# A two-layer hybrid decoder trunk: the layer and unit loops, written out in the instruction streams or run as hardware loops

## The reference

```python
for l in range(DEPTH):
    h = rmsnorm(x, norm_w[l])
    proj = jnp.einsum('bld,dn->bln', h, w_in[l]).astype(f32)
    ...
    y_a = gdn_branch(...)        # gated DeltaNet, 8 heads of 128
    y_b = hgrn2_branch(...)      # HGRN2, 8 heads of 128
    y_c = s5_branch(...)         # S5 state space, 64 groups of 16 channels
    y_d = retention_branch(...)  # RetNet retention, 8 heads of 128
    branch = jnp.einsum('blcw,cwd->blcd', ys, w_branch[l]).astype(f32)
    gates = jax.nn.sigmoid(gate_logits.reshape(B, L, N_BRANCH, D_MODEL))
    merged = jnp.sum(gates * branch, axis=2)
    x = x + jnp.einsum('bld,de->ble', merged.astype(x.dtype), w_out[l])
return rmsnorm(x, final_norm_w)
```

## Time and profile before

| | before |
|---|---|
| time, median of 3 runs | 3149.24 us |
| profiled execution: its own time | 3147.71 us |
| profiled execution: span from first to last instruction | 3145.9 us |
| PE busy | 3036.6 us (97%), granted clock 0.995 |
| DVE busy | 2167.7 us (69%) |
| ACT busy | 1461.4 us (46%) |
| POOL busy | 270.1 us (9%) |

### The profile page before, as it was taken

The page is one execution under the profiler, slowest core; times in us unless marked ns, Lnnn a source line. Parts: engine busy times, 40 slices in busy tenths (PEclk is TensorE's granted clock), DMA queues, the critical chain, the costliest instruction groups (busy, mean ns, idle before and its releaser), DMA issues.

```text
span 3145.9 us, 50828 instructions
## 1 busy us (share of the span) xinstructions
PE 3036.6 (97%) x20316; PEld 2769.8 (88%) x20316; DVE 2167.7 (69%) x3300; ACT 1461.4 (46%) x2102; POOL 270.1 (9%) x512
## 2 busy tenths in 40 slices
PE   5999999999999999999989999999999999999998
PEld 5999999999998888888889999999999988888886
DVE  5877877887786555545558877877877865555554
ACT  4455355445536444444453555455355454444443
POOL 2012102101200000000011011012102000000000
PEclk9999999999999999999989999999999999999999
DMA  4455445455546666666634455455445566666655
GB/s 125 133 142 141 133 132 145 130 136 138 145 128 189 194 194 194 193 195 187 203 98 134 126 144 136 130 138 151 125 135 139 146 195 194 194 193 193 193 178 167
DMA packets 614108, 494.23 MB, mean 157 GB/s; under 512 B 18512, under 2 KB 496272, under 8 KB 613360
## 3 DMA queue, kind: packets, MB, share of 16 engines
q1 hardware_dynamic: 606800, 485.09, 53.7%
q0 software_dynamic: 6784, 4.70, 0.7%
q10 hardware_dynamic: 288, 1.18, 0.1%
HBM read 488.81 MB, written 2.10 MB: 156 GB/s over the span
## 4 chain that ended last, share of the span: by engine, by line
PE 43%; issue 24%; DVE 18%; DVEq 7%; ACT 6%; ACTq 2%; DMA 0%; SPq 0%; POOLq 0%; POOL 0%
PE PJ L1431 24%; PE S L1431 6%; DVE w_lo L969 5%; PE GA L1431 3%; PE RA L1431 3%; PE HA L1431 3%; PE GB L1431 2%; DVE region L1112 2%; DVEq L1087 2%; DVE work L1085 2%; ACT w_hi L553 2%; DVEq L1142 1%; DVEq L1137 1%; DVE mix L1065 1%; DVEq L1105 1%
## 5 line engine op out<-in xcount | busy, mean ns | idle before, releaser
L969 DVE TENSOR_TENSOR w_lo<-raw_w,w_hi 128x1024 fp32r<-128x1024 f32 x912 | 1115.6, 1224 | 767.6 <-ACT w_hi L553 742.6
L553 ACT ACTIVATE w_hi<-raw_w 128x1024 fp32r<-128x1024 f32 x912 | 964.3, 1059 | 822.4 <-PE PJ L1431 377.8
L1431 PE MATMUL PJ<-h_hi,w_hi 128*128 128x256 f32 x3584 | 1045.8, 292 | 0.0
L1431 PE MATMUL PJ<-h_hi,w_lo 128*128 128x256 f32 x3584 | 1015.2, 283 | 0.0
L1431 PE MATMUL PJ<-h_lo,w_hi 128*128 128x256 f32 x3584 | 1014.8, 283 | 0.0
L1431 PEld LDWEIGHTS PJ<-h_hi,w_hi 128*128 128x128 f32 x3584 | 688.0, 192 | 11.9 <-issue 11.9
L1431 PEld LDWEIGHTS PJ<-h_lo,w_hi 128*128 128x128 f32 x3584 | 688.4, 192 | 0.0
L1431 PEld LDWEIGHTS PJ<-h_hi,w_lo 128*128 128x128 f32 x3584 | 687.0, 192 | 0.0
L1431 PE MATMUL PJ<-w_hi,h_hi 128*128 128x512 f32 x640 | 249.2, 389 | 2.0 <-DVE h_lo L1363 2.0
L1431 PE MATMUL PJ<-w_hi,h_lo 128*128 128x512 f32 x640 | 249.0, 389 | 0.0
L1431 PE MATMUL PJ<-w_lo,h_hi 128*128 128x512 f32 x640 | 249.0, 389 | 0.0
(11 more groups left out here) (398 smaller groups left out, 4235.5 us busy)
## 6 DMA issues: line engine op xcount, KB each, us to landing
raw_w<-w_in SPq DMA_DIRECT2D x704, 512.0 KB, 3.7
raw_w<-w_branch SPq DMA_DIRECT2D x128, 512.0 KB, 4.2
raw_w<-w_out SPq DMA_DIRECT2D x64, 512.0 KB, 4.2
raw_w<-s_glu_w SPq DMA_DIRECT2D x16, 512.0 KB, 4.7
ret_decay<-c_ret POOLq DMA_DIRECT2D x16, 128.0 KB, 3.2
work<-final_norm_w SPq DMA_DIRECT2D x2, 1024.0 KB, 7.3
out<-x_tok SPq DMA_DIRECT2D x4, 512.0 KB, 2.9
x_tok<-x ACTq DMA_DIRECT2D x1, 1024.0 KB, 7.9
```

What stands on the lines that cost most here:

```text
L553: A_(w_hi[i % RING][:, :, :], raw_w[i % RING][:, :, :], ACT.Copy).then_inc(hi_ready, 1)
L969: TT(w_lo[i % RING][:, :, :], raw_w[i % RING][:, :, :], w_hi[i % RING][:, :, :].bitcast(f32), ALU.subtract).then_inc(raw_used[i % RING], 1)
L1431: return nc.tensor.matmul(o, w, m, start=start, stop=stop)
```

## The change

The Python loops over layers and over units become hardware loops on all five engines. The counts and offsets that were constants are now registers (`snap` puts an expression into one). The bodies are the same, and so is the work that is executed.

```diff
@@ SP
-            for l in range(DEPTH):
-                r0 = l * RAW_USES
+            with sp.Fori(0, DEPTH) as l:
+                r0 = sp.snap(l * RAW_USES)
...
-                for u in range(UNITS):
-                    base = r0 + u * USES
+                with sp.Fori(0, UNITS) as u:
+                    base = sp.snap(r0 + u * USES)
...
@@ ACT
-                for u in range(UNITS):
-                    n = l * UNITS + u
-                    n1 = n + 1
-                    s0, r0 = sl + u * HALVES, rl + u * USES
-                    ga0, gb0 = n * GA_N, n * GB_N
-                    ha0, sa0, cv0 = n * HA_N, n * SA_N, n * 3
+                with act.Fori(0, UNITS) as u:
+                    n = act.snap(l * UNITS + u)
+                    n1 = act.snap(n + 1)
+                    s0, r0 = act.snap(sl + u * HALVES), act.snap(rl + u * USES)
+                    ga0, gb0 = act.snap(n * GA_N), act.snap(n * GB_N)
+                    ha0, sa0, cv0 = act.snap(n * HA_N), act.snap(n * SA_N), act.snap(n * 3)
...
@@ PE
-                for u in range(UNITS):
+                with pe.Fori(0, UNITS) as u:
...
-                p0, pr, q0 = sl + POST_SPLIT0, rl + UNITS * USES, l * STEPS
+                p0, pr, q0 = pe.snap(sl + POST_SPLIT0), pe.snap(rl + UNITS * USES), pe.snap(l * STEPS)
```

More of the change, by code:

```diff
@@ L379, in _ @@
                         load(i, base, W[ds(l, 1), :, k0:k0 + HALF, ds(u * P + BLOCKS[i // 2], P)])
-                post = r0 + UNITS * USES
+                post = sp.snap(r0 + UNITS * USES)
                 def load_wide(i, source):
@@ L424, in _ @@
             pool.dma_start(log_dt[:, :], A["s5_log_dt"].rearrange("l (j g) -> (l j) g", g=2)).then_inc(s5_in, 16)
-            for l in range(DEPTH):
-                l1 = l + 1
+            with pool.Fori(0, DEPTH) as l:
+                l1 = pool.snap(l + 1)
                 pool.wait_ge(params_used, l1)
@@ L448, in _ @@
                 nc.gpsimd.tensor_tensor(x_rs[:, :], x_rs[:, :], mhalf[:, 0:2], ALU.pow).then_inc(rms_ready, 1)
-                for u in range(UNITS):
-                    n1 = l * UNITS + u + 1
+                with pool.Fori(0, UNITS) as u:
+                    n1 = pool.snap(l * UNITS + u + 1)
                     pool.wait_ge(bc_used, n1)
@@ L553, in split_hi @@
                 A_(w_hi[i % RING][:, :, :], raw_w[i % RING][:, :, :], ACT.Copy).then_inc(hi_ready, 1)
-            for l in range(DEPTH):
-                l1 = l + 1
-                sl, rl = l * SPLITS, l * RAW_USES
+            with act.Fori(0, DEPTH) as l:
+                l1 = act.snap(l + 1)
+                sl, rl = act.snap(l * SPLITS), act.snap(l * RAW_USES)
                 split_hi(0, sl, rl)
@@ L767, in _ @@
                     ahead(27)
-                p0, pr = sl + POST_SPLIT0, rl + UNITS * USES
-                q0 = l * STEPS
+                p0, pr = act.snap(sl + POST_SPLIT0), act.snap(rl + UNITS * USES)
+                q0 = act.snap(l * STEPS)
                 def ahead(j):
@@ L970, in split_lo @@
                    ALU.subtract).then_inc(raw_used[i % RING], 1)
[L972 to L975, removed]
+            with dve.Fori(0, DEPTH) as l:
+                l1 = dve.snap(l + 1)
+                a0 = dve.snap(l * 2)
+                sl = dve.snap(l * SPLITS)
                 mean_square(l1)
@@ L1049, in _ @@
                 dve.drain().then_inc(cols_ready, 1)
[L1051 to L1055, removed]
+                with dve.Fori(0, UNITS) as u:
+                    n = dve.snap(l * UNITS + u)
+                    n1 = dve.snap(n + 1)
+                    ga0, gb0, ha0 = dve.snap(n * GA_N), dve.snap(n * GB_N), dve.snap(n * HA_N)
+                    ra0, sa0, cv0 = dve.snap(n * RA_N), dve.snap(n * SA_N), dve.snap(n * 3)
                     def tap(m, k):
@@ L1068, in conv_taps @@
                         last.then_inc(conv_summed, 1)
-                    s0 = sl + u * HALVES
+                    s0 = dve.snap(sl + u * HALVES)
                     def ahead(i):
@@ L1339, in y_low @@
                     last.then_inc(y_lo_ready, 1)
-                p0, q0 = sl + POST_SPLIT0, l * STEPS
+                p0, q0 = dve.snap(sl + POST_SPLIT0), dve.snap(l * STEPS)
                 def ahead(j):
@@ L1447, in three_pass @@
                 return MM(o, wl, mh, False, last)
-            for l in range(DEPTH):
-                l1 = l + 1
-                sl, rl = l * SPLITS, l * RAW_USES
+            with pe.Fori(0, DEPTH) as l:
+                l1 = pe.snap(l + 1)
+                sl, rl = pe.snap(l * SPLITS), pe.snap(l * RAW_USES)
                 pe.wait_ge(params_in, l1 * (16 * 11))
@@ L1458, in _ @@
                 pe.wait_ge(diag_ready, l1)
-                x0 = l * (KT // 2)
+                x0 = pe.snap(l * (KT // 2))
                 def scale_x(i):
@@ L1492, in _ @@
                 MM(RA[:, 2 * UNITS:3 * UNITS], after, gate_g[:, 0, :]).then_inc(gc_written, 1)
[L1493 to L1498, removed]
+                with pe.Fori(0, UNITS) as u:
+                    n = pe.snap(l * UNITS + u)
+                    n1 = pe.snap(n + 1)
+                    pj0, ga0, gb0, ha0 = pe.snap(n * NB), pe.snap(n * GA_N), pe.snap(n * GB_N), pe.snap(n * HA_N)
+                    ra0, sa0, cv0 = pe.snap(n * RA_N), pe.snap(n * SA_N), pe.snap(n * 3)
+                    r0 = pe.snap(rl + u * USES)
                     def project(i):
```

## The result

The changed kernel takes 3240.78 us (median of 4 runs, 3238.36 to 3244.29) against 3149.53 us before (4 runs, 3147.71 to 3150.5): a ratio of 1.0287, 95% interval 1.0275 to 1.0299, so 91 us slower. The forecast was 3195 us, 46 us slower. The profiled execution took 3245.19 us, with a span of 3243.5 us, 97.6 us more than that of the kernel before. Its time is the second longest, and its mean granted clock of 0.988 the lowest, of 26 executions on record (3233.88 to 3245.33 us, clock 0.988 to 0.994), so what is read from its trace is some 4 us more than the median shows.

The account below looks back on a forecast made before the run. PE bounds the kernel, paced by DVE for some 47 us of each unit. Terms 29 + 3 + 2 + 10 + 4 = 48 us on 3147.71 gave 3196, forecast 3195 us; range 3154 to 3262, forecast's own 3180 to 3220.

Parts of the forecast that it names:

- rival 1: Unit starts: each code fetch exposed with 5 us on PE, or other engines late; 3257 us (3220 to 3290), chance 0.20.
- The register rows on DVE: L1094 to the second rotary part: register rows directly behind drains cost 1.8 us a unit, 29 us in all.
- counts from registers: Instructions waiting for a register's value cost extra at dispatch: 0.2 us, 3 us in all.
- PE's rows: Register rows on PE, covered by its sequencer's 2.0 us lead: nothing; without cover 3.5 us a unit.
- ACT and the table load: ACT, 504 to 527.6 us: moved load gains 0.2 us, two tap rows on DVE cost 0.3; 2 us in all.
- The way back: Branch to a unit's start: code fetch outlasts PE's lead, 0.7 us each, 15 times, 10 us.
- The cautious end of my forecast: Upper figure for PE's loss at each branch back to a unit's start: 2.0 us.
- Both delays run side by side, so the larger counts: Unit starts: PE's loss of 0.7 to 2.0 us and DVE's 0.5 us lateness overlap; 0.7 us taken.
- Layer starts: Serial stretch between engines at each layer's start, with branch and ISA rows: 2 us each, 4 us.
- Wide stage, SP and POOL: SP's loads wait for `w_lo`, POOL is ready 7.2 us early, wide stage has no idle to grow: nothing.
- my own signs against me: Wrong if units grow under 1 us, growth sits at their starts, or PE's busy time changes.
- rival 2: Unit loop's code is still held, no stall at the branch; 3184 us (3165 to 3190), chance 0.20.

Follow-up runs that it names:

- e6: Kernel before with DVE alone given the layer loop, its eight units written out, counts in registers; 3168.43 us, ratio 1.0069.
- e5: Changed kernel with the prefetch hint for the unit loop's closing branch on PE, DVE and ACT; 3183.50 us, ratio 1.0118.
- e4: Changed kernel with the unit loops of PE, DVE, ACT and POOL written out inside the layer loop; 3172.67 us, ratio 1.0075.
- e10: Kernel before with PE alone looped, with the prefetch hint for its unit loop's closing branch; 3151.32 us against 3148.64, ratio 1.0008.
- e8: Kernel before with ACT alone looped; 3147.81 us against 3147.07, ratio 1.0002.
- e1: Kernel before with PE's instruction stream alone looped, without a hint; 3203.92 us, ratio 1.0171.
- e3: Changed kernel with the prefetch hint for the unit loop's closing branch on PE alone; 3204.11 us, ratio 1.0176.
- e7: Kernel before with DVE alone looped over layers and units; 3196.77 us, ratio 1.0158.
- e12: Kernel before, no loop, with 45 already fulfilled waits on PE at the start of each unit but a layer's first; 3199.52 us, ratio 1.0159.
- e11: Kernel before, no loop, with 75 already fulfilled waits on PE at the start of each unit but a layer's first; 3268.45 us, ratio 1.0382.
- e2: Changed kernel with PE's stream written out, while DVE, ACT, POOL and SP loop; 3201.02 us, ratio 1.0168.

## Why the prediction was half right

The direction and the place of one half were right. The time was 46 us short and above the forecast's own range, 3180 to 3220 us, in that of rival 1, 3220 to 3290 us. Nearly all of the 46 us is one term of the sum. (The sum itself gave 3196 us on the profiled execution and so 3197 on the median, not 3195, and rival 1's 113 us make 3262 and not 3257; neither changes the account.)

*The register rows on DVE, 29 us, and counts from registers, 3 us.* Measured: 22 us for the rows of the counts (e6), and some 13 us, give or take 7, for the rows that the unit number adds (e5 less e4, 0.0043 of 3149), 35 us for the forecast's 32. That they come so close is in part luck. In the stretch that I had priced, the waits after `h_scores` and the rotary parts went from 31.1 to 50.1 us at PE, 19 us for my 29, and the 13 us lie mostly at the taps, outside that stretch. There is growth also in the GA of the decay (3.6 to 10.1 us), which I had not named. The rows themselves are 40 ns (ALU_OP) and 57 ns (FUSED_REGOPS, median) on DVE. Before L1128, where a FUSED_REGOPS row of 46 ns took the place of the semaphore's row of 21 ns, the idle time went from 3.0 to 3.6 us, 0.04 us for each of 16.

*PE's rows, nothing.* Right: at most 5 us (e10).

*ACT and the table load, +2 us.* Right as nothing: 0.6 us [-2 to 3] (e8). The win of 0.2 us a unit is there in e8's wait GB <- ACT region L631, 5.8 us for 8.5 in 16, but not in its time, and in the changed kernel this wait is 9.5. One thing was mis-sized: I had 0.3 us a unit for two rows between the taps. There are nine, and the idle time at them grew by 0.76 us a unit (22.0 against 9.8 us, over 16), counted above.

*The way back, 10 us: the step that failed in size.* I wrote "with some 0.3 us for branch and register rows and a lead of 2.0 us, PE loses between 0.7 and 2.0 us" and took 0.7 times 15. The form of this sum holds, and 14 times is the right count. The fetch is the wrong term: I took 2.4 us from the landing of an 8 KB load, where the branch with its fetch is 4.5 us. So it is 2.8 us each, 39 us, and 17 us more for what follows it (next part). The cautious end of my forecast, 2.0, lay below too, though the 5 us of rival 1 were above.

*What was missing.* The clock. Nowhere had I asked what PE's engine does after standing still. Eight stretches of half clock, 40.8 us: the matmuls follow each other there by 0.21 us in place of 0.12,

```profile
643.54 0.58 PE L1431 MATMUL PJ<-h_hi,w_hi 128*128 128x256 f32 x1 [2.88 <-issue]
643.92 0.41 PE L1431 MATMUL PJ<-h_lo,w_hi 128*128 128x256 f32 x1
644.13 0.41 PE L1431 MATMUL PJ<-h_hi,w_lo 128*128 128x256 f32 x1
644.35 0.41 PE L1431 MATMUL PJ<-h_hi,w_hi 128*128 128x256 f32 x1
```

so that at most 40.8 x (1 - 0.12/0.21) = 17 us are lost in this execution. With the stops that is 56 us for the 10 of the forecast, and e1 less e10 says 51 on the chip.

*"Both delays run side by side, so the larger counts."* Right, and the runs show it: PE alone looped costs 54 us, DVE alone 50, together 104; less the 13.7 us that show at GB only once PE's stop is gone (e3), 90, which is the 91 measured. DVE was later than my 0.5 us, with two stops, but hidden.

*Layer starts, 4 us.* Half of it: the first GB of layer 1 comes at 66.06 in place of 65.01 us, and from the last S matmul of the wide stage to the first GB of layer 2 it is 39.25 us in place of 38.49, together 1.8 us. No row stood behind my 2 us each. From the first GB of the eighth unit to the wide stage it is 2.2 us more in layer 1 and 2.5 us in layer 2, with no way back in between. *Wide stage, SP and POOL, nothing.* Right.

The sum as measured: 35 on DVE, 39 for stops, 17 for the clock, 2 for the layers is 93 us, against 97.6 of the spans. Rival 1 came nearest in time (3257 us), and of its two forms it was the fetch on PE, not the late engines. Of my own signs against me, two of three came: the growth sits at the units' starts for more than half, and PE's busy time changed.

The Trainium skill, page "Runtime: NRT & Kernel Launch", section "Instruction fetch mechanics", says that a taken branch to a page outside the current two stalls on a fetch. The trace agrees for PE (4.5 us) and DVE (3.0 us behind the branch). ACT's next row came after 0.2 us, and the packets fit that: with ACT alone looped (e8) q14 has 16 between 200 and 900 us for 23 before, with DVE alone looped (e7) 41. ACT's unit has 188 rows in the trace and is not fetched again, DVE's has 312 and is. The same section of the Trainium skill also says that prefetch is purely sequential and only two lines are held. The hinted loop contradicts that: 700 us without a packet on q8, over more than six units of some 1800 instructions each. My rival 2, code that is held, is thus right for a loop with a hint and wrong for one without. Why the same code is fetched again without a hint was not tried.

## What to carry to other kernels

Price a hardware loop engine by engine: a register row on the engine that paces counts (some 90 rows a unit on DVE cost 2.2 us of it), a row on an engine with a full queue cost next to nothing (at most 5 us of 3149 on PE), and a branch back to code that must be fetched again cost 4.5 us on PE, less the 2.0 us that its queue was ahead, and 3.0 us and a second stop on DVE. On ACT, whose unit is short, it cost nothing. Arm the hint on every engine that paces or is waited for, since the hint on PE alone gave back 37 us and those on DVE and ACT 20 more; with all three the loops still cost 37 us. After each stop of PE look at the granted clock: here a stop of 2.8 us cost 3.7 us on average (51 us over 14), and part of that is in no list of waits.

## What the runs showed of the hardware

- The clock: in the changed kernel it went from 1.00 to 0.50 (of 2.4 and 1.2 GHz the lower) behind eight of fourteen stops of 2.8 us, in e12 behind nine stops of the same length without a loop, in e11 behind all fourteen of 6 us. It differs between executions of the same kernel: the changed kernel's mean clock was 0.988 at 3245.19 us and 0.994 at 3233.88 us. In e2 and e3, whose waits at the unit's first GB are at most 1.2 and 1.1 us, it stayed at 1.00 in the units; in e7, with stops of up to 1.3 us there, it fell twice, for 3.4 us each. Why one stop of 2.8 us is followed by half clock and the next is not, these runs don't tell.
- A branch's record is no measure of its cost: on PE it holds the fetch (4.5 us), on DVE it is 63 ns and the 3.0 us stand behind it. With the hint PE's is 0.22 us. The Trainium skill, page "Advanced Engine Details and Errata", section "Control Flow Timing", has about 108 ns for a compare-and-branch; the rows here have 45 ns (ACT), 63 ns (DVE) and 216 ns (PE, with the hint).
- Each way back of PE without a hint brought two packets more than the straight code (190 for 161 on q8, 14 ways back), and with it none after the first unit.
- Two fulfilled waits in one row on PE take 51 ns by the record and 106 ns from row to row.
